# Transformer block in fp32 pairs on one core: RWKV matmuls sorted by tile shape, a gate panel's split moved into the GELU, and inverse and attention steps interleaved in another order

## The reference, cut to what matters

```python
def hybrid_mixer(h, ...):            # T = 256 positions, 1024 channels
    proj = h @ w_in                  # rw, sc, sg, sb columns and 4 x 1024 gate columns
    y_a = short_conv_mixer(proj[sc])
    y_b = stick_breaking_attention(q, k, v)          # 4 heads
    y_c = rwkv7_mixer(proj[rw], ...)                 # 4 heads, 2 chunks of 128
    y_d = spatial_gating(proj[sg], ...)              # gelu, layer norm, causal mix
    gates = sigmoid(proj[gate] + gate_b)             # four of 1024 columns
    merged = sum(gates[b] * (y_b @ out_b) for b in range(4))
    return merged @ w_o

# rwkv7, per head: S_t = S_{t-1} diag(w_t) + (S_{t-1} a_t) b_t^T + v_t k_t^T ; y_t = S_t r_t
# first_block: x += mixer(norm(x)); x += conv_glu_ffn(norm(x)); norm
# second_block: two layers of pooling or window attention, memory attention and MLP
```

## Time and profile before

| What | us |
|---|---|
| median of 3 runs (1018.68 to 1023.67) | 1020.57 |
| the profiled execution, its own time | 1017.16 |
| its span, first to last instruction | 1015.3 |
| PE busy in the span | 988.9 |
| DVE busy | 697.9 |
| ACT busy | 537.3 |
| POOL busy | 35.5 |
| mean of one whi copy on ACT (155) | 1.909 |
| mean of one wlo subtraction on DVE (155) | 2.291 |

### The profile page before, as it was taken

The page is one execution under the profiler, slowest core; times in us unless marked ns, Lnnn a source line. Parts: engine busy times, 40 slices in busy tenths (PEclk is TensorE's granted clock), DMA queues, the critical chain, the costliest instruction groups (busy, mean ns, idle before and its releaser), DMA issues.

```text
span 1015.3 us, 20609 instructions
## 1 busy us (share of the span) xinstructions
PE 988.9 (97%) x8640; PEld 956.4 (94%) x8640; DVE 697.9 (69%) x863; ACT 537.3 (53%) x689; POOL 35.5 (3%) x28
## 2 busy tenths in 40 slices
PE   6998999999999999998999999999999999999998
PEld 5998898998999999998978999999999899999998
DVE  5668755655788988998885755556776867555553
ACT  5465655446565555455744544444576665434432
POOL 0025050000000000000000000000000000000000
PEclk9999999999999999998999999999999999999999
DMA  7643433233645565455243556646633135565461
GB/s 269 214 169 118 163 125 117 93 126 117 261 175 185 197 214 204 144 197 204 86 130 120 188 186 207 207 165 207 207 129 134 72 126 192 182 207 207 165 207 42
DMA packets 24833, 168.97 MB, mean 166 GB/s; under 512 B 2752, under 2 KB 3264, under 8 KB 4800
## 3 DMA queue, kind: packets, MB, share of 16 engines
q1 hardware_dynamic: 24192, 165.82, 46.9%
q10 hardware_dynamic: 576, 2.20, 0.6%
HBM read 166.96 MB, written 1.05 MB: 165 GB/s over the span
## 4 chain that ended last, share of the span: by engine, by line
PE 79%; DVE 14%; ACT 5%; issue 2%; DMA 0%; DVEq 0%; ACTq 0%
PE G L595 13%; PE G L597 13%; PE G L596 13%; PE D L595 8%; PE D L597 8%; PE D L596 8%; DVE wlo L1784 5%; PE M L595 2%; PE M L597 2%; PE M L596 2%; ACT whi L1265 2%; PE M L812 1%; PE D L1166 1%; PE M L642 1%; PE D L1193 1%
## 5 line engine op out<-in xcount | busy, mean ns | idle before, releaser
L1784 DVE TENSOR_TENSOR wlo<-raw,whi 128x2048 fp32r<-128x2048 f32 x155 | 354.3, 2291 | 122.8 <-ACT whi L1265 122.6
L595 PE MATMUL G<-xh,whi 128*128 128x256 f32 x1280 | 361.6, 282 | 4.4 <-DVE xl L1805 2.9
L596 PE MATMUL G<-xl,whi 128*128 128x256 f32 x1280 | 355.0, 277 | 0.0
L597 PE MATMUL G<-xh,wlo 128*128 128x256 f32 x1280 | 355.0, 277 | 0.0
L1265 ACT ACTIVATE whi<-raw 128x2048 fp32r<-128x2048 f32 x155 | 295.5, 1909 | 50.5 <-PE D L597 47.4
L595 PEld LDWEIGHTS G<-xh,whi 128*128 128x128 f32 x1280 | 240.7, 188 | 12.5 <-DVE wlo L1784 7.2
L596 PEld LDWEIGHTS G<-xl,whi 128*128 128x128 f32 x1280 | 240.7, 188 | 1.3 <-issue 1.2
L597 PEld LDWEIGHTS G<-xh,wlo 128*128 128x128 f32 x1280 | 240.7, 188 | 0.0
L595 PE MATMUL D<-hh,whi 128*128 128x256 f32 x672 | 185.8, 277 | 0.8 <-issue 0.8
L597 PE MATMUL D<-hh,wlo 128*128 128x256 f32 x672 | 185.7, 276 | 0.0
L596 PE MATMUL D<-hl,whi 128*128 128x256 f32 x672 | 185.6, 276 | 0.0
(11 more groups left out here) (399 smaller groups left out, 1394.2 us busy)
## 6 DMA issues: line engine op xcount, KB each, us to landing
raw<-wall_dram SPq DMA_DIRECT2D x155, 1024.0 KB, 4.9
x<-x_dram SPq DMA_DIRECT2D x4, 256.0 KB, 5.3
mem<-mem_dram ACTq DMA_DIRECT2D x1, 1024.0 KB, 5.1
out_dram<-x SPq DMA_DIRECT2D x4, 256.0 KB, 2.2
poolw<-pool_w_dram ACTq DMA_DIRECT2D x1, 768.0 KB, 6.6
cst<-cst_dram SPq DMA_DIRECT2D x1, 448.0 KB, 12.3
lora<-lora_dram SPq DMA_DIRECT2D x1, 256.0 KB, 11.7
sgw<-sg_w_dram SPq DMA_DIRECT2D x1, 256.0 KB, 12.5
```

Of the source, the lines that this page charges most:

```text
L595: mm(out, w_h, hi, start=start, stop=False, skip_group_check=skip)
L596: mm(out, w_h, lo, start=False, stop=False, skip_group_check=skip)
L597: return mm(out, w_l, hi, start=False, stop=stop, skip_group_check=skip)
L1784: signal(tt(wlo[:, pan.slot, 0:w], raw[:, pan.slot, 0:w], f32(whi[:, pan.slot, 0:w]), SUB), "w_lo")
```

## The change

Four places of the code. (1) In `rw_out` and `rw_rhs` the loops over heads are split, so that matmuls of one tile shape stand together; the accumulation flags follow. (2) ACT and DVE each call `split_to(PAN["gate0"] + 1)` within `sg_gelu`, so the first gate panel is split there, before ACT's tanh and before DVE's wait for it. (3) `sg_mean` goes from ahead of the convolution to behind the first half of gate0.0, `sg_var` behind the second half, the first attention steps and `rw_prod` 0 one slot later. (4) An RWKV step is put in its slot at index 1, behind the first attention step there, and not at the end; since an attention entry is a pair such as `sb_z`, `sb_e`, the RWKV step now stands between the two.

```diff
--- before.py
+++ after.py
@@ -347,7 +347,7 @@
     W += [("rw_low",), ("panel", PAN["sc"]), ("rw_gates",), ("panel", PAN["sc"] + 1), ("rw_cum",), ("rw_square",),
           ("panel", PAN["sc"] + 2), ("panel", PAN["sg"]), ("rw_key",), ("panel", PAN["sg"] + 1), ("rw_scale",), ("rw_mix",),
           ("panel", PAN["sb"]), ("sg_gelu",), ("panel", PAN["sb"] + 1), ("rw_turn",),
-          ("panel", PAN["sb"] + 2), ("sg_mean",), ("sc",), ("ahead_lo", PAN["sb"] + 2)]
+          ("panel", PAN["sb"] + 2), ("sc",), ("ahead_lo", PAN["sb"] + 2)]
     rw = [("rw_prod", i) for i in range(4)] + [("inv_first",)]
     for g in range(1, len(JOINS)):
         rw += [("inv_t", g)] + [("inv_p", g, k) for k in range(1, POWERS[g] + 1)]
@@ -368,18 +368,20 @@
 
     held = [i for i in range(len(slots)) if i + 1 < len(slots) and WHAT[slots[i + 1][1]][0] in OUTS]
     put = {i: [] for i in range(len(slots))}
-    put[0].append(("sg_var",))
-    put[2] += sbs.pop(0)
+    put[0].append(("sg_mean",))
+    put[1].append(("sg_var",))
     put[3] += sbs.pop(0)
-    room = [i for i in range(4, slots.index(("panel", PAN["out2"]))) if i not in held]
+    put[4] += sbs.pop(0)
+    room = [i for i in range(5, slots.index(("panel", PAN["out2"]))) if i not in held]
     for k, steps in enumerate(sbs):
         put[room[k * len(room) // len(sbs)]] += steps
-    room = [i for i in range(3, len(slots)) if i not in held][:-RW_ENDS]
+    room = [i for i in range(4, len(slots)) if i not in held][:-RW_ENDS]
     joined = [[step] for step in rw]
     joined[joined.index([("inv_first",)])].insert(0, ("rw_rhs", 0))
     assert len(joined) <= len(room)
     for k, steps in enumerate(joined):
-        put[room[k]] += steps
+        first = len(put[room[k]]) if k == 0 else 1
+        put[room[k]][first:first] = steps
     for i, f in enumerate(slots):
         W.append(f)
         W += put[i]
@@ -872,14 +874,14 @@
                 pe.wait_ge(S("rw_prod"), 8)
             else:
                 pe.wait_ge(S("rw_state"), 1)
+            outs = [M[h % 2][:, 0, (h // 2) * 64:(h // 2 + 1) * 64] for h in range(4)]
             for h in range(4):
+                ins = mm(outs[h], gm[:, 4 * ch + h, 2, :], vn[:, ch, h * 64:(h + 1) * 64],
+                         start=h < 2, stop=ch == 0, skip_group_check=True)
+            for h in range(4 if ch else 0):
                 j, o = h // 2, 64 * (h % 2)
-                out = M[h % 2][:, 0, j * 64:(j + 1) * 64]
-                ins = mm(out, gm[:, 4 * ch + h, 2, :], vn[:, ch, h * 64:(h + 1) * 64],
-                         start=True, stop=ch == 0)
-                if ch:
-                    ins = mm(out, ar[o:o + 64, 2 * j + ch, 0, :], st[o:o + 64, j, :],
-                             start=False, stop=True)
+                ins = mm(outs[h], ar[o:o + 64, 2 * j + ch, 0, :], st[o:o + 64, j, :],
+                         start=False, stop=True, skip_group_check=True)
             ins.then_inc(S("rw_rhs"), 1)
             freed["M0"] = freed["M1"] = ("rw_b0", 2 * ch + 2)
 
@@ -910,14 +912,20 @@
 
             pe.wait_ge(S("rw_uu"), 2)
             pe.wait_ge(S("rw_bonus"), 1)
-            for h in range(4):
-                j, o = h // 2, 64 * (h % 2)
+            for j in range(2):
                 for ch in range(2):
-                    out = DB[2][o:o + 64, j, ch * P:(ch + 1) * P]
-                    mm(out, uu[:, ch, h, :], gm[:, 4 * ch + h, 1, :], start=True, stop=False)
-                    ins = mm(out, vn[:, ch, h * 64:(h + 1) * 64], gm[:, 4 * ch + h, 3, :], start=False, stop=ch == 0)
-                    if ch:
-                        ins = mm(out, st[o:o + 64, j, :], ar[o:o + 64, 2 * j + ch, 1, :], start=False, stop=True)
+                    for o in (0, 64):
+                        h = 2 * j + o // 64
+                        mm(DB[2][o:o + 64, j, ch * P:(ch + 1) * P], uu[:, ch, h, :], gm[:, 4 * ch + h, 1, :],
+                           start=j == 0 and ch == 0, stop=False, skip_group_check=True)
+                    for o in (0, 64):
+                        h = 2 * j + o // 64
+                        mm(DB[2][o:o + 64, j, ch * P:(ch + 1) * P], vn[:, ch, h * 64:(h + 1) * 64], gm[:, 4 * ch + h, 3, :],
+                           start=False, stop=ch == 0, skip_group_check=True)
+            for j in range(2):
+                for o in (0, 64):
+                    ins = mm(DB[2][o:o + 64, j, P:2 * P], st[o:o + 64, j, :], ar[o:o + 64, 2 * j + 1, 1, :],
+                             start=False, stop=True, skip_group_check=True)
             ins.then_inc(S("rw_yp"), 1)
 
         def rw_gn1():
@@ -1493,6 +1501,7 @@
             projected(act, "sg", 1)
             signal(fn(sgt[:], z_sg[:], ACT.Square), "sg_z2")
             tables("exp_and_others")
+            split_to(PAN["gate0"] + 1)
             act.wait_ge(S("sg_z3"), 1)
             signal(fn(sgt[:], sgt[:], ACT.Tanh, scale=math.sqrt(2.0 / math.pi)), "sg_e")
 
```

## The result

The changed kernel takes 1027.49 us (median of 10 runs, 1023.63 to 1034.55) against 1019.38 for the kernel before (10 runs, 1014.17 to 1023.92): ratio 1.0084, 95% interval 1.0055 to 1.0113, so some 8.6 us slower. The forecast was +4.2 us; the time lies in its range, 1021 to 1028, the change is twice as large. That the time lies in the range is in part luck: the kernel before came to 1019.38 in this measurement, and the forecast had started from 1020.57. From there, 8.6 us more would be 1029.2. The profiled execution took 1030.17 us.

A forecast was written before the change was run, and what follows sets the result against it. TensorE (PE) bounds the mixer stage. New waits 14.2, less 9.9 gained, plus 0.2 for shape changes gave +4.5 us, the queue walk +4.1; taken +4.2: profiled 1017.2 to 1021.4, median 1024.8, range 1021 to 1028.

The forecast's parts named there:

- The sort: rw_out and rw_rhs of chunk 1: sorted matmuls save 2.9 and 1.3 us, 4.2 in all; 1.7 if only shape changes count.
- Rival C: Sorted matmul pairs don't overlap, so only shape changes are saved, 1.7 for 4.2: 1027.3 us, slower; chance 0.1.
- sg_var: Variance's sum: PE, back at 97.9, waits 1.3 us for DVE's centring and ACT's squares, ready by 99.1.
- sg_turn: PE waits 1.3 us for the normed value, its Ln queued on ACT behind a panel copy, two tanh and a table load.
- first gate panel: gate0's first panel, low part moved ahead of the tanh wait: PE starts at 91.5; two waits removed, worth 2.35 us.
- out0: PE waits 2.2 us for gate0.3's bank; sb_a 0, a panel copy and a table load precede its tanh on ACT.
- inv_first: PE waits 0.9 us for ix, GpSimd's inm being slowed beside DVE's low part; the 0.6 wait for b stays.
- out1: PE waits 2.3 us, as in out0: sb_e 2 stands before gate1.3's tanh on ACT.
- out3: PE waits 2.0 us for a low part after gn2's late Ln, then 1.0 for gate3.3's tanh and 0.8 on DVE.
- A: Steps keep their slack: new waits don't arise, 9.9 us gained less 0.2, 1010.9 us; chance of faster 0.2.
- B: out3's chain is longer, pushing the stage's end by half a panel (2.9 us): 1027.7 us, slower; chance 0.2.
- D: The forecast itself: 1021 to 1025.7 us, with the half-size-waits middle, counted as same; chance 0.5.

The follow-up runs named there:

- The run without alternation: Kernel before with rw_out and rw_rhs 1 matmuls sorted by tile shape, column or row halves not alternated: 1013.21 us, ratio 0.9942.
- sorted kernel: Kernel before with only the new loops of rw_rhs and rw_out, old order and slots: 1011.41 us, ratio 0.9939.
- Filling the gap: Changed kernel with five useless 256-column matmuls on PE ahead of inv_first's wait for ix: 1024.65 us, ratio 1.0053.
- shortening the wait: Changed kernel with DVE's low part of gate1.1 and GpSimd's next-level masks put behind ix: 1021.78 us, ratio 1.0038.
- kernels with late slots: Kernels keeping the change's one-slot-later steps, such as the changed kernel without interleave: 1020.10 us, ratio 1.0024.
- old slots: Steps in the kernel before's slots, as in sorted + interleave (1016.09 us, ratio 0.9982) and sorted + GELU (1015.97 us, 0.9983).
- four chosen places: Sorted kernel with inv_p 2 1, inv_b, rw_prod 2 and rw_rhs 0 each ahead of an attention step: 1011.10 us, ratio 0.9912.
- last kernel of the ix series: Changed kernel with DVE's low part of gate1.1 and GpSimd's next-level masks behind ix: 1021.78 us, ratio 1.0038.
- sorted + interleave kernel: Kernel before with the sorted steps and the RWKV interleave, old slots and old GELU: 1016.09 us, ratio 0.9982.
- kernel with two places: Sorted kernel with only inv_p 2 1 put ahead of sb_e 2 and inv_b ahead of sb_a 3: 1011.33 us, ratio 0.9909.

## Why the prediction came out as it did

*The sort:* right in size (4.2 forecast, 4.3 measured), wrong in part of the reason. I split it into shape changes, 1.7, and pairs by alternation, 2.5. The run without alternation still gave 3.7: sorting by shape is enough to let the two column halves run side by side, and strict alternation adds 0.6. Rival C rested on the same split. The Trainium skill's rule of different row tiles and one PSUM bank (TensorEngine Tiling, Restrictions and Gotchas) was not borne out: the four state products take 0.65 us in every sorted order, where in line, at 0.22 each, they would take 0.9. That 0.22 is the price of 128*64 tiles with the same 128 columns; no run shows 64*64 tiles in line.

*The new waits, place by place* (forecast, measured): sg_var 1.3, 0.2; sg_turn 1.3, 1.1; first gate panel 0.4, which the forecast took off the waits gone, 1.3; sb_q 0 1.8, 1.4; out0 2.2, 2.4; inv_first 0.9 beside the old 0.6, 3.3; out1 2.3, 2.1; inv_b 0.6, 0.6; out3 2.0 + 1.0 + 0.8, 1.3 + 0.7 + 0.5. The sum of the forecast's new waits, 14.8 with the old 0.6, was 14.9. The idle time of PE rose by 8.9 us; the forecast's waits less those gone (14.2 - 5.1) say 9.1. So the walk of the queues was right about who waits for whom in seven of nine places. That the sum fits so closely is luck: 1.1 too much at sg_var and 1.3 at out3 stand against 1.3 that was missing at the first gate panel and 1.8 at inv_first. The first gate panel waits because DVE's low part took 3.40 us instead of 2.2; the rows have it beside the convolution on GpSimd, which before ran beside steps of the GELU (no run separates the two):

```profile
87.79 3.40 DVE L1793 TENSOR_TENSOR wlo<-raw,whi 128x2048 fp32r<-128x2048 f32 x1
```

*The step that failed* stands in the first line of the working: "I use the clock of the profile before." Every duration behind a wait was taken at 2.4 GHz. The clock fell behind the waits for ix and for out1's sig, 2.7 + 1.6 = 4.3 us that no term held. Filling the gap and shortening the wait both give back the 2.7 of the first place; the 1.6 of out1 are read from the trace alone. The forecast's walk, +4.1, and 4.3 make 8.4; measured were 10.3. The last 1.9 are mostly busy time of PE: 1.4 more than the sorted kernel's once the clock is taken off, where I had 0.2 for shape changes. PE's start times say where it is. A wait in the middle of a panel stretches the matmuls beside it: around out0's, the last one before starts 0.28 us ahead of the wait and the first one behind stands for 0.22, where others stand 0.115 apart. The changed kernel has six such waits and the sorted one has one, which makes 1.2 us; the other kernels with late slots have five or six, those with old slots one. And the panels' matmuls stand 0.1160 us apart on average in this profile's stage against 0.1154 in the sorted kernel's, 0.5 us over the stage; that is the pair of speeds described at the end, and no effect of the change.

*inv_first* was also mis-sized as a wait. ix came at 143.3, the very time of the forecast, but that is a coincidence: in this profile the stage starts at 82.78, and in the one that the forecast counted from at 84.13. Counted from the start of the stage, ix came 1.4 us late, since its masks gm ended 0.6 later and ix itself took 2.25 instead of 1.39, and PE stood there 0.4 us earlier than forecast. The forecast had the low part slowing inm but ix at its own speed.

*The rivals:* A was wrong, the waits did arise. B gave 1027.7, very near the 1027.5 measured, but by a tail longer than the forecast's 3.8, and the tail was 2.5: the right number for a wrong reason. D was the right mechanism without the clock.

## What to carry to other kernels

When PE is the bound, price a new wait of several us twice: as the wait, and as matmuls behind it at half clock, here up to 2.8 us more. It came behind each wait of 3.3 and 3.8 us, behind some of 1.9 to 2.4, and once behind two of 1.3 and 1.1. So a step order is judged by its longest waits too, and not only by their sum. Put a step in front only where PE waits for its own result, and look at what it pushes back: the same edit made everywhere cost 4 to 6 us and at four chosen places gained 3.6. And before starting a GpSimd operation next to DVE's critical one, see whether both read SBUF: moving work that nobody waits for took 3 us off without touching PE's program.

## What the hardware showed beyond that

DVE and GpSimd can slow each other: inm takes 1.17 us alone and 2.5 to 3.3 beside a low part, ix 1.39 alone and 2.25 beside inm, a low part 2.29 and 3.40. Not always both: the low part at 136.53 started before inm and took its usual 2.28, and the inm behind it took 2.51. The Trainium skill states the rule (SBUF — State Buffer, Who interferes with whom): a DVE instruction with two inputs in SBUF contends with a GpSimd instruction that reads SBUF, and the port pair that they share is an exclusive lock; these rows agree with it.

The fall of the clock does not follow from the length of one wait alone. Behind 3.3 and 3.8 us it fell in each profile that has them, behind 1.9 and 2.0 at inv_first as well, behind 1.09 not. But out0's 2.4 brought it down only in the last kernel of the ix series, and there out1's 2.07 did not; nor did the 2.5 at `sb_q` 3 in the sorted + interleave kernel. Yet in that kernel it fell at 94 to 98 us, behind two waits of 1.3 and 1.1 that five other profiles have without a fall. That may be part of why runs of one kernel differ.

PE also has two speeds at a granted clock of 1.00. Windows of 50 us, full of panels, in the changed kernel:

```profile
360.00:410.00 50.00, 50.00 (x427) 50.00 (x426) 41.41 (x58) 25.17 (x33) 0.00 (x0) 1.00 0.55 189
...
610.00:660.00 50.00, 50.00 (x444) 50.00 (x443) 27.33 (x19) 21.70 (x18) 0.00 (x0) 1.00 0.58 194
```

427 or 444 matmuls in the same time, 117 or 113 ns each, without a wait in either. The slower speed can last long: here from 310 to 460 us, which makes some 5.5 us of this execution's 1030.17; in the profiled execution of the kernel with two places from 610 us to its end, some 14 us, which is why that one took 1023.63 while its fastest run took 1008.58. The sorted kernel's profile has it only in short stretches, as from 98 to 103 us within the stage, where the panel's matmuls stand 0.118 us apart. So the stage is not quite free of it: by the mean spacing of its panel matmuls it makes up to 0.7 us between these kernels, so a difference of stage of that size needs the rows of its own place. Since only profiled executions show it, I can't say how much of the spread between runs it makes; it is why the stage in the trace tells more here than the time of one execution.
